# The last two output blocks of an MLP by Strassen's identity as well, and products of Strassen's identity summed in one PSUM bank

## The reference, cut to what matters

```python
def sq_relu_mlp(h, w1, w2):           # h 256 x 2048, w1 2048 x 8192, w2 8192 x 2048
    a = jax.nn.relu(h @ w1)
    return (a * a) @ w2

x = x + sq_relu_mlp(rms_norm(x, g), w1, w2)
```

## Time and profile before

| | |
|---|---|
| median of 3 runs | 2095.98 us |
| the profiled execution's own time | 2096.38 us |
| its span | 2094.6 us |
| TensorE busy | 2088.4 us, 10850 matmuls |
| VectorE busy | 1560.2 us (74%) |
| ScalarE busy | 1144.0 us (55%) |
| granted TensorE clock | 1.00 |
| mean DMA rate | 197 GB/s |

### The profile page before, as it was taken

How to read it: one execution, slowest core, us unless ns; L and a number is a source line. 1 busy time by engine, 2 the same in 40 slices (tenths; PEclk the granted TensorE clock), 3 DMA queues, 4 the chain that set the end, 5 groups by cost and what they waited for, 6 DMA issues and landing times.

```text
span 2094.6 us, 27475 instructions
## 1 busy us (share of the span) xinstructions
PE 2088.4 (100%) x10850; PEld 1765.6 (84%) x10850; DVE 1560.2 (74%) x2067; ACT 1144.0 (55%) x1425; POOL 53.6 (3%) x44
## 2 busy tenths in 40 slices
PE   9999999999999999999999999999999999999999
PEld 8888888888887888888788888888888888888887
DVE  7798787777778867768875566556778688688775
ACT  6777565565564555665555445454545445444452
POOL 0000000000000000000010011000000000000000
PEclk9999999999999999999999999999999999999999
DMA  8565555564554744447564554455576666566663
GB/s 324 194 239 191 195 210 191 200 211 178 205 192 150 247 160 146 157 151 231 191 211 171 189 181 171 164 181 203 200 221 212 209 221 199 219 188 198 241 181 141
DMA packets 67425, 411.82 MB, mean 197 GB/s; under 512 B 7392, under 2 KB 14304, under 8 KB 19808
## 3 DMA queue, kind: packets, MB, share of 16 engines
q1 hardware_dynamic: 64992, 393.28, 52.3%
q0 software_dynamic: 2304, 16.78, 4.4%
HBM read 407.80 MB, written 2.23 MB: 196 GB/s over the span
## 4 chain that ended last, share of the span: by engine, by line
PE 99%; DVE 1%; ACT 0%; issue 0%; POOL 0%
PE bank L1146 27%; PE bank L1168 15%; PE bank L1170 15%; PE bank L1172 15%; PE bank L1151 14%; PE bank L1188 2%; PE bank L1184 2%; PE bank L1186 2%; PE bank L1266 1%; PE bank L1401 1%; PE bank L1337 1%; PE bank L1359 0%; PE bank L1389 0%; PE bank L1268 0%; PE bank L1296 0%; PE bank L1245 0%
## 5 line engine op out<-in xcount | busy, mean ns | idle before, releaser
L1893 DVE TENSOR_TENSOR wlo<-raw,whi 128x2048 fp32r<-128x2048 f32 x314 | 718.5, 2289 | 217.6 <-ACT whi L1461 186.9
L1461 ACT ACTIVATE whi<-raw 128x2048 fp32r<-128x2048 f32 x314 | 600.2, 1912 | 250.9 <-PE bank L1172 230.7
L1146 PE MATMUL bank<-A,whi 128*128 128x512 f32 x2448 | 587.7, 392 | 0.0
L1146 PEld LDWEIGHTS bank<-A,whi 128*128 128x128 f32 x2448 | 451.1, 188 | 91.8 <-issue 2.4
L1151 PEld LDWEIGHTS bank<-A,wlo 128*128 128x128 f32 x2432 | 311.8, 191 | 11.8
L1151 PE MATMUL bank<-A,wlo 128*128 128x256 f32 x2432 | 315.3, 283 | 0.0
L1168 PE MATMUL bank<-whi,A2h 128*128 128x512 f32 x768 | 301.2, 392 | 0.0
L1170 PE MATMUL bank<-whi,A2l 128*128 128x512 f32 x768 | 299.3, 390 | 0.0
L1172 PE MATMUL bank<-wlo,A2h 128*128 128x512 f32 x768 | 299.1, 389 | 0.0
L1168 PE MATMUL bank<-whi,A 128*128 128x512 f32 x608 | 241.7, 398 | 0.0
L1170 PE MATMUL bank<-whi,A 128*128 128x512 f32 x608 | 237.2, 390 | 0.1
(11 more groups left out here) (267 smaller groups left out, 1897.6 us busy)
## 6 DMA issues: line engine op xcount, KB each, us to landing
raw<-wst SPq DMA_DIRECT2D x308, 1024.0 KB, 4.8
W<-wst SPq DMA_DIRECT2D x37, 1024.0 KB, 4.9
W<-wst POOLq DMA_DIRECT2D x10, 1024.0 KB, 8.3
W<-cum_scratch SPq DMA_DIRECT2D x8, 1024.0 KB, 7.0
raw<-wst POOLq DMA_DIRECT2D x6, 1024.0 KB, 8.0
W<-rows SPq DMA_DIRECT2D x21, 256.0 KB, 5.9
W<-first SPq DMA_DIRECT2D x12, 384.0 KB, 7.6
W<-exp_scratch SPq DMA_DIRECT2D x16, 256.0 KB, 6.4
```

What stands on the lines that cost most here:

```text
L1146: last = e.matmul(o[:, :], whi[:, s, k * P:(k + 1) * P], A1[:, k, :, :].rearrange("p h t -> p (h t)"), start=k == 0, stop=packed and k == ...
L1461: e.activation(whi[:, u % 3, :], raw_of(u), ACT.Copy).then_inc(*hi.inc((u, 3)))
L1893: e.tensor_tensor(wlo[:, u % 3, :], raw_of(u), whi[:, u % 3, :], ALU.subtract).then_inc(*lo.inc((u, 3)))
```

## The change

1. `plan()`: in section 3 the pair (2, 3) of output blocks gets its seven products a to g too, and down 2.2, 2.3, 3.2, 3.3 are gone. The fourteen products and eight plain units of the last section stand in a new order, which has two products for one plain unit from product c on.
2. Everywhere (all eight groups, and the new one): a, d and f are accumulated in one PSUM bank. d starts with `start=False` onto a, and f onto a + d. VectorE drains the bank after a, after d and after f, and d may not start before a's drain, nor f before d's. ScalarE's copy of a and VectorE's two additions onto it are gone, in each group. Drains of a group go from 11 VectorE instructions and one of ScalarE to 9 of VectorE.

```diff
     def down(s, nbs):
         return [("B", ("down", s, nb, i), "mlp_w2_2", 16 * s + 4 * i, nb * 512) for nb in nbs
-                for i in range(2 if seven(s, nb) else 4)]
+                for i in range(2)]
...
-        u += in_turn("-a-c-b-d-e-f-g", sevens("dp", "mlp_w2_2", s, 0), down(s, (1, 0, 2, 3)))
+        if s < QT - 1:
+            u += in_turn("-a-c-b-d-e-f-g", sevens("dp", "mlp_w2_2", s, 0), down(s, (1, 0, 2, 3)))
+        else:
+            u += in_turn("-a-cb-d-ef-ga-cb-d-efg", sevens("dp", "mlp_w2_2", s, 0) + sevens("dp", "mlp_w2_2", s, 1),
+                         down(s, (1, 0, 3, 2)))
...
     left, right = pair_of(tag)
-    return {"a": (), "b": ((1, right, 1), (0, right, 1)), "c": ((0, right, 1),),
-            "d": ((0, left, 1), None, (0, right, -1)), "e": ((0, left, 1),), "f": (None, (1, right, -1), (1, left, 1)),
-            "g": ((1, left, 1),)}[tag[3]]
+    return {"a": ((0, left, 1),), "b": ((1, right, 1), (0, right, 1)), "c": ((0, right, 1),), "d": ((0, right, -1),),
+            "e": ((0, left, 1),), "f": ((1, right, -1), (1, left, 1)), "g": ((1, left, 1),)}[tag[3]]
...
-                    e.matmul(o, h, wh, start=name in ("a", "b", "d", "f") and k == 0, stop=False)
+                    e.matmul(o, h, wh, start=name in ("a", "b") and k == 0, stop=False,
+                             skip_group_check=name in ("d", "f"))
...
+                elif form == "P" and tag[3] in "df":
+                    BEFORE[u, t] = evac_v, (product(u, "a" if tag[3] == "d" else "d"), 0)
...
-                if form == "P" and tag[3] == "a":
-                    w.wait_ge(*mm_done(u))
...
-                    e.activation(kept(u), bank[BANK[u, 0]][:, :], ACT.Copy).then_inc(*keep_a.inc(u))
...
-                if not DRAINS[u, n]:
-                    w.wait_ge(*(evac_v((u, 0)) if tag[3] == "d" else evac_v((product(u, "d"), 2))))
-                    e.tensor_tensor(kept(u), ps, kept(u), ALU.add).then_inc(*evac_v.inc((u, n)))
-                    return
```

More of the change, by code:

```diff
@@ L318, in shut @@
 def shut(tag):
-    if tag[0] == "down" and seven(tag[1], tag[2]):
+    if tag[0] == "down":
         return (1,) if tag[2] % 2 and tag[3] == 1 else ()
@@ L342, in block_of @@
     left, right = pair_of(tag)
-    return {"c": (s, right, 0), "e": (s, left, 0), "g": (s, left, 1)}.get(name, (u,))
+    return {"c": (s, right, 0), "e": (s, left, 0), "g": (s, left, 1), "b": (u,)}.get(name, ("sum", s, p))
 def pieces12(x, n):
@@ L684, in stack_kernel @@
             "nv": lambda j, h: na_v(f"l{h}", j), "upb": lambda t: upb_v(("l", t)),
-            "bp": lambda x: keep_a(bp["a"]) if x == "a" else evac_v((bp[x], {"b": 1, "d": 1, "f": 0}[x])),
+            "bp": lambda x: evac_v((bp["f" if x == "a" else x], 1)),
         }
@@ L739, in side_uses @@
                 yield ("upb", r[0]), r[0]
-            elif what == "mm" and units[r[0]][1][0] == "bp" and units[r[0]][1][3] in "abdf":
+            elif what == "mm" and units[r[0]][1][0] == "bp" and units[r[0]][1][3] in "ab":
                 yield ("bp", units[r[0]][1][3]), None
@@ L748, in stack_kernel @@
                 SIDE[use], side_before[b] = (b, side_before[b]), use
-        for x in "abdf":
+        for x in "ab":
             BANK[bp[x], 0] = 4 + SIDE["bp", x][0]
             BEFORE[bp[x], 0] = None, SIDE["bp", x][1]
+        for x, before in (("d", "a"), ("f", "d")):
+            BANK[bp[x], 0] = BANK[bp["a"], 0]
+            BEFORE[bp[x], 0] = evac_v, (bp[before], 0)
         def side_free(use):
@@ L774, in stack_kernel @@
             u, n = key
[L775 to L778, removed]
+            PIECE[key], PIECES[piece[:2]] = PIECES.get(piece[:2]), key
+            EMPTIED[block_of(u, units[u][1], n if units[u][0] == "B" else 0)] = key
         for x in "abcdefg":
             DRAINS.update({(bp[x], n): piece for n, piece in enumerate(drains(units[bp[x]][1]))})
-        FIRST = ((bp["c"], 0), (bp["d"], 0), (bp["f"], 2))
-        LAST = {(bp["d"], 2): (0, 2), (bp["e"], 0): (0, 1), (bp["f"], 1): (1, 2), (bp["g"], 0): (1, 1)}
+        FIRST = ((bp["c"], 0), (bp["a"], 0), (bp["f"], 1))
+        LAST = ((bp["d"], 0), (bp["e"], 0), (bp["f"], 0), (bp["g"], 0))
         pool = [[holds[i][0] + 1, evac_v if units[holds[i][0]][1][0] not in ON_ACT else evac_a, holds[i]]
@@ L1183, in product_block @@
                     wh, wl = (x[:, u % 3, k * 512:(k + 1) * 512] for x in (whi, wlo))
-                    e.matmul(o, h, wh, start=name in ("a", "b", "d", "f") and k == 0, stop=False)
+                    e.matmul(o, h, wh, start=name in ("a", "b") and k == 0, stop=False,
+                             skip_group_check=name in ("d", "f"))
                     w.wait_ge(*low_made)
-                    e.matmul(o, low, wh, start=False, stop=False)
+                    e.matmul(o, low, wh, start=False, stop=False, skip_group_check=name in ("d", "f"))
                     w.wait_ge(*lo((u, 3)))
-                    last = e.matmul(o, h, wl, start=False, stop=k == 3)
+                    last = e.matmul(o, h, wl, start=False, stop=k == 3, skip_group_check=name in ("d", "f"))
                 last.then_inc(*mm.inc((u, 0)))
```

27 lines of the change are left out of this document (5 added, 22 removed).

## The result

The changed kernel takes 2101.2 us (median of 12 runs, 2100.39 to 2103.49) where the kernel before takes 2096.1 (12 runs beside it, 2095.78 to 2096.77): a ratio of 1.0023, 95% interval 1.0016 to 1.0031. It is slower by 5.1 us; 2102.0 was forecast. The profiled execution took 2101.39 us.

A forecast was written before the change was run, and what follows sets the result against it. TensorE's count of matmuls bounds the kernel as long as tiles are split in time. -2.7 + 6.7 + 2.0 = +6.0 us on the profiled 2096.4 gives 2102.4, less 0.4 for the runs' median: 2102.0 us, range 2097.0 to 2107.0.

The forecast's parts named there:

- Saved on TensorE: Last section: four plain units (96 matmuls) go, seven products (84) come; 12 x 0.2276 = 2.7 us saved.
- Drains: Per group, ScalarE's copy and two VectorE additions go; worth 0 ahead of the last section, new waits there 0 too.
- The walk: Last section traced unit by unit: TensorE waits at eight places for late weights, 6.7 us in sum.
- The landing of b's DMA: Last group: b's accumulating DMA lands after 10.1 us, not 8.1, slowed by loads behind it; +2.0 us.
- The clock: Rival: waits of 1 to 4 us in TensorE's stream drop it to 1.2 GHz; 2107 to 2110 us; chance 0.05.
- d', down 2.1 and g': Last group, behind b': separate TensorE waits of 1.0, 0.8 and 0.9 us, added into the sum.
- The signs named: What the new profile should show: eight waits from the first d on, most at b', its DMA landing after 9 to 11 us.

The follow-up runs named there:

- Order two: Changed kernel with the last section's units in order a--b-cdA-fe-gB-C-D-EFG (capitals: pair (2, 3), dash: plain unit); 2093.9 us.
- The fill: Changed kernel with 14 extra matmuls on data at hand ahead of product b of the last group; 2103.3 us.
- loads behind b held: Changed kernel with the two plain loads issued behind b's accumulating DMA (last group) held back until it has landed; 2100.6 us.
- b not added: Changed kernel where the DMA bringing b's second tile in the last group overwrites the tile instead of adding to it; 2097.3 us.
- small adds in the first group: Changed kernel with VectorE's adds for d and g of the last section's first group over 8 columns instead of 2048; 2097.7 us.
- small adds in the last group: Changed kernel with VectorE's adds of weight tiles for d and g of the last group over 8 columns instead of 2048; 2099.9 us.
- load ahead held: Changed kernel where the plain load issued 3.0 us ahead of b's accumulating DMA, and those behind it in SyncE's queue, wait until that DMA has landed; 2102.3 us.
- second group only: Kernel before with the second group of seven products in the changed kernel's order, products still drained with the kept copy in SBUF; 2102.6 us.
- order two with the kept copy: Order two, but products drained as in the kernel before (kept copy in SBUF, no running sums in PSUM); 2095.8 us.
- order one: Changed kernel with the last section's units in order a--cb--Ad-egfB-C-D-EGF (capitals: pair (2, 3), dash: plain unit); 2094.8 us.

## Why the prediction was right, step by step

- **Saved on TensorE, 2.7 us: right.** Order two shows it almost alone.
- **Drains, 0 us: right ahead of the last section** (the sums in PSUM alone, 2096.4). In the last section they are worth 1.4 us against a kept copy; the walk had them in it, since it counted no additions.
- **The walk, 6.7 us of waits and 2.0 of DMA: the sum nearly right (8.1), its split not.** Primes mark the pair (2, 3) as in the prediction. Measured at d 0.24 (forecast 0.2), down 0.1 0.7 (0.8), a' 0.6 (0.6), b' 3.55 (2.3 + 2.0), down 2.0 0 (0.1), d' 0 (1.0), down 2.1 0.3 (0.8), g' 0.6 (0.9). To these 6.1 us come 1.6 of slow clock, which the walk did not have, and 0.4 of matmuls standing a little over 0.2276 us apart. Up to a' the walk is right to 0.1 us.
- **The landing of b's DMA, 10.1 us: 9.7, and the reason is not borne out.** I blamed the two loads behind it. With both behind it, it landed after 8.1 us in another kernel, and after 10.7 in a trace with both held back. So that this term came out 0.4 us from its size is luck; what made it 9.7 stays open. Nor was 8.1 us the figure of DMAs with the engines nearly to themselves: 12 of the 16 in the kernel before had a plain load ahead of them still under way, and the four without one landed after 8.0 to 9.1.
- **The clock: a rival at 0.05, and it fell.** Behind waits of 1.5 and 1.8 us inside one product it was at half (1.2 GHz) for 3.5 us. The rival's price (a product more, 2.7 us, two or three times) was wrong: 1.6 us, once. The Trainium skill (TensorE: Matmul & The Clock Gate, "Why this matters for your kernels") warns of gaps between bursts; here the trace agrees, with 0.66 in the five microseconds after two gaps close together and 1.00 with the first one filled. The fill gave no time back, so I take it that these 1.6 us did not move the end.
- **d', down 2.1 and g' as terms of their own: the step that was loose.** Behind b' the end is one chain, 26.5 us from b's high part to the start of g's low part in the changed kernel and in three more traces (loads behind b held, b not added, small adds in the first group), with a slow clock or without. So TensorE's losses there (slow clock or waits) are not added; they take each other's place. The walk from low b' on had just that chain (low down 2.0, add d', splits, f', add g') and put the end of low g' at 2093.1 + 1.6 us of later landing, 2094.7, where it ended at 2093.75. Of this 1 us the chain itself is 0.5 (29.3 us to the end of low g' in the walk, 28.8 measured), the earlier start of the section 0.4. The forecast was 1.0 us too high for the profiled execution (2102.4 against 2101.4): 0.4 for the landing, 0.4 for that start, which is chance, and the rest for the chain.
- **The signs named.** Waits only from d on: yes, at six of the eight places. b' the largest: yes. The DMA of b' landing after 9 to 11 us: 9.7. DMA issued 0.6 us after low a': 0.55. d' and g' reached while ScalarE waits for an add: no. It waits 5.7 us for the add of d', but the high part is done before TensorE, late from b', comes there; g' waits for its low part alone. The clock ahead of down 1.0: unchanged at 1.00; the time: 0.4 us less, which I put down to chance.

Not settled: why this DMA lands after 8 us at one time and 10 at another, the times of the fill kernel above its profile, and which of order two's moves matters most (only whole orders were run).

## What to carry to other kernels

Removing TensorE work at the end of a kernel can move the bound to what prepares its operands; then add up the preparing engine's time between the last event it can't move (here a DMA's landing) and the last matmul, and compare that one chain with TensorE's time, instead of summing waits one by one. A change that saves 12 matmuls and loses 5 us can be a good change in a bad order: try to spread the units that need most preparation, and to start long transfers several units ahead of their use, as the two orders did here together. A trace is one execution: see where it stands among the runs before you build on a time in it. If a clock drop follows a wait, first ask who sets the end; where it isn't TensorE, as here, filling the wait may bring nothing.

## What the runs showed of the hardware

- The granted clock fell to half (1.2 GHz) for some 3.5 us behind waits close together in TensorE's stream. These are, in excess: 1.5 and 1.8 us in the changed kernel and with small adds in the last group, 2.6 and 1.8 with the loads behind b held, and 1.8, 0.6 and 1.8 with the load ahead held. In two traces where waits of 1.8 us stood by themselves (second group only, two of them 26 us apart; small adds in the first group, one), and in one with a wait of 1.6 (order two with the kept copy), it stayed at 1.00.
- With a load ahead under way for 3.8 us more, a plain copy of 1 MB from GpSimd's queue landed after 7.3 us (one transfer); six accumulating ones with 3.3 to 4.8 us to go, all in the last section, took 9.7 to 10.9. The plain loads of SyncE take 4.8 in the median. Two accumulating DMAs issued 1.8 us apart (order one) landed after 7.7 and 10.8.
- Plain loads issued behind an accumulating DMA that is under way take longer: 9.7 and 11.2 us in the changed kernel, 8.3 and 10.1 with the second group only; without one under way the same two took 4.8 and 6.8.
- Some kernels that wait for that DMA scatter more: 2098.0 to 2104.1 (small adds, last group) and 2100.6 to 2104.8 (fill), against 2093.5 to 2096.0 in order two.
